# A two-layer hybrid attention and long-convolution step on one core: transposes, chunk order and handovers rearranged, two modulation chunks formed on another engine

## The reference

```
mod = silu(cond) @ w_ada + b_ada; sh1, sc1, g1, sh2, sc2, g2 = split(mod, 6)
h = x * (1 + sc1) + sh1
q, k, v, z, gate_a, gate_b = split(h @ w_in)
attn = softmax with a sink over |i-j| <= 128 (latent queries also read all context keys), rotary on q, k
x0, x1, u = split(depthwise_conv3(z)); g = the implicit filter of the layer, from a small sine MLP
hy = x0 * (irfft(rfft(x1 * u) * rfft(g)) + bias * (x1 * u))
merged = sigmoid(gate_a) * (attn @ w_pa) + sigmoid(gate_b) * (hy @ w_pb)
x = layer_norm(alpha * x + g1 * (merged @ w_out))
gate, val = split((x * (1 + sc2) + sh2) @ w_up)
x = layer_norm(alpha * x + g2 * ((gelu(depthwise_conv3(gate)) * val) @ w_down))
```

## Time and profile before

| quantity | value |
|---|---|
| median of 3 runs | 2078.3 us (2069.81 to 2085.46) |
| the profiled execution | 2079.39 us |
| its span | 2077.6 us |
| mean granted TensorE clock | 0.990 |

### The profile page before, as it was taken

How to read it: one execution, slowest core, us unless ns; L and a number is a source line. 1 busy time by engine, 2 the same in 40 slices (tenths; PEclk the granted TensorE clock), 3 DMA queues, 4 the chain that set the end, 5 groups by cost and what they waited for, 6 DMA issues and landing times.

```text
span 2077.6 us, 30343 instructions
## 1 busy us (share of the span) xinstructions
PE 2021.1 (97%) x13030; PEld 1920.9 (92%) x13030; DVE 1144.3 (55%) x1678; ACT 747.4 (36%) x1099; POOL 183.3 (9%) x202
## 2 busy tenths in 40 slices
PE   8999999999999999999999999999999999999997
PEld 3588998999989999999998999799998999999996
DVE  6416556867565777767544555763346533233435
ACT  3444344522255331233234444362226332133323
POOL 0120001200033000000022000120014000000011
PEclk9999989999999999999999999999999999999998
DMA  8331113245412435443322101222221221222121
GB/s 311 143 126 58 39 42 112 71 152 184 142 61 82 163 119 196 163 162 134 112 84 82 48 35 62 93 75 71 96 83 41 82 75 57 90 74 81 63 71 51
DMA packets 37726, 207.07 MB, mean 100 GB/s; under 512 B 4326, under 2 KB 7959, under 8 KB 18904
## 3 DMA queue, kind: packets, MB, share of 16 engines
q1 hardware_dynamic: 31192, 185.04, 24.8%
q0 software_dynamic: 3312, 13.35, 1.8%
q10 hardware_dynamic: 3088, 6.75, 0.9%
HBM read 196.98 MB, written 8.14 MB: 99 GB/s over the span
## 4 chain that ended last, share of the span: by engine, by line
PE 89%; DVE 4%; ACT 3%; issue 2%; DMA 1%; POOL 1%; SPq 0%; ACTq 0%; DVEq 0%; POOLq 0%
PE gemm_psum L608 50%; PE gemm_psum L638 15%; PE gemm_psum L661 4%; PE gemm_psum L681 3%; PE aux_psum L740 3%; PE gemm_psum L621 2%; PE aux_psum L793 2%; PE gemm_psum L550 2%; PE gemm_psum L779 2%; PE aux_psum L727 1%; PE gemm_psum L514 1%; PE aux_psum L763 1%; PE aux_psum L717 1%; DMA ada_early<-in_ada 1%; DVE scores L1626 1%
## 5 line engine op out<-in xcount | busy, mean ns | idle before, releaser
L608 PE MATMUL gemm_psum<-h_hi,w_hi 128*128 128x322 f32 x2176 | 504.6, 313 | 0.2 <-DVE gate_acc L1763 0.2
L608 PE MATMUL gemm_psum<-h_hi,w_lo 128*128 128x322 f32 x2176 | 500.8, 311 | 0.0
L608 PE MATMUL gemm_psum<-h_lo,w_hi 128*128 128x322 f32 x2176 | 498.9, 310 | 0.0
L1558 DVE TENSOR_TENSOR w_lo<-w_raw,w_hi 128x2048 fp32r<-128x2048 f32 (+4 forms) x134 | 260.4, 1943 | 218.2 <-ACT w_hi L1087 217.2
L608 PEld LDWEIGHTS gemm_psum<-h_hi,w_hi 128*128 128x128 f32 x2176 | 368.0, 189 | 4.7 <-issue 3.8
L608 PEld LDWEIGHTS gemm_psum<-h_lo,w_hi 128*128 128x128 f32 x2176 | 367.7, 189 | 0.0
L608 PEld LDWEIGHTS gemm_psum<-h_hi,w_lo 128*128 128x128 f32 x2176 | 367.4, 189 | 0.0
L1087 ACT ACTIVATE w_hi<-w_raw 128x2048 fp32r<-128x2048 f32 (+4 forms) x134 | 217.2, 1621 | 170.4 <-PE gemm_psum L638 65.6
L1546 DVE CUSTOM_DVE_ANT_0 aux_psum<-w_raw,cond_by_row 128x1024 f32<-128x1024 f32 x160 | 190.9, 1255 | 4.5 <-DMA w_raw<-in_ada_t 4.3
L1692 DVE SCALAR_TENSOR_TENSOR x<-gemm_psum,mod,x 128x128 f32<-128x128 f32 (+2 forms) x144 | 55.4, 434 | 160.6 <-PE gemm_psum L638 130.9
L638 PE MATMUL gemm_psum<-act_hi,w_lo 128*128 128x322 f32 x616 | 141.9, 311 | 0.0
(11 more groups left out here) (323 smaller groups left out, 3253.5 us busy)
## 6 DMA issues: line engine op xcount, KB each, us to landing
w_raw<-in_w_up SPq DMA_DIRECT2D x44, 1024.0 KB, 4.8
w_raw<-in_ada_t SPq DMA_DIRECT2D x40, 1024.0 KB, 4.7
w_raw<-in_w_down SPq DMA_DIRECT2D x32, 704.0 KB, 4.1
w_raw<-in_w_gate SPq DMA_DIRECT2D x16, 1024.0 KB, 4.7
w_raw<-in_w_z SPq DMA_DIRECT2D x12, 1024.0 KB, 4.7
w_raw<-in_w_out SPq DMA_DIRECT2D x8, 1024.0 KB, 4.7
g_kept<-g_rows_out POOLq DMA_DIRECT2D x10, 512.0 KB, 2.9
ada_early<-in_ada SPq DMA_DIRECT2D x4, 1024.0 KB, 20.6
```

What stands on the lines that cost most here:

```text
L608: last = mm(gp[:, 2 * (t % 2) + hf, 0:HALF], w[:, off + P * kk:off + P * (kk + 1)], moving(kk, lo)[:, hf * HALF:(hf + 1) * HALF], start=kk ...
L1558: TT(wlo[s][:, 0:n], raw[STEP[(lane.layer, "g", g)] % 2][:, 0:n], f32(whi[s][:, 0:n]), ALU.subtract).then_inc(sem["w_split"], raised("w_sp ...
```

## The change

1. Chunks 6 and 7 of layer 0's first modulation are no longer matmuls on PE but eight products on DVE, between filter products. The stream order becomes 6, 4, 7, 5. Twelve transposes stay, and the last four columns of the second vector come from the products. The products go to a new SBUF tile, one behind the other.
2. The load of `cond_rows` moves from POOL's queue to ACT's, ahead of x's two, and its Silu from the attention part to between the filters.
3. Six rows of layer 1's filter spectra (from the fifth on) are emptied by DVE, not ACT, around the split of chunk 0, and several rows of ACT's copies are moved into the loop that makes h.
4. Chunks 1 and up1 are split in halves too.
5. Three heads of p are transposed ahead of z's second tile (two before); in the last block, which has one z tile, that tile is done in halves, with the transposes between. ACT copies p of heads 0 and 2 ahead of z's second tile. `attn_lo` of the block before comes after the score maxima, not among them.
6. Pair 0's spectrum goes to two banks of its own, `spectrum(2)` waits no more for `usp_out`, and `attn_projected(1)` does; `early_row(0)` and `(2)` move behind splits of y.
7. At LN1 the statistics of the second half come after six channel groups (four before), with splits, squares and sums in another order on ACT, DVE and POOL.

The core of the diff:

```diff
-    order = [(0, "pre", 0), (0, "pre", 1)] + [(0, "ada", s) for s in range(ADA_EARLY, ADA_FIRST)]
+    order = [(0, "pre", 0), (0, "pre", 1)] + [(0, "ada", s) for s in (6, 4, 7, 5)]
-HALVED = [0] + [at_g("gate", m) for m in range(1, EARLY + 1)] + [at_g("up", 0)]
+HALVED = [0, 1] + [at_g("gate", m) for m in range(1, EARLY + 1)] + [at_g("up", 0), at_g("up", 1)]
+    spec_bank = lambda r: ax[:, r, :] if r < 2 else gp[:, r % 4, :]
@@ PE, opening @@
-        filter_rows(1, 4, 6)
+        filter_rows(1, 4, 8)
         ada(4)
+        filter_rows(1, 8, 10)
         g_spectrum(0, 1)
-        filter_rows(1, 6, 8)
+        g_spectrum(0, 2)
         ada(5)
-        g_spectrum(0, 2)
-        filter_rows(1, 8, 10)
-        ada(6)
-        ada(7)
         g_spectrum(1, 0)
-        pe.wait_ge(sem["row_first"], 4)
+        pe.wait_ge(sem["row_first"], 3)
-        for t in range(2 * KD):
+        for t in range(2 * ADA_ROWS):
@@ PE, attention @@
-                tile(5 + b, 0, KD, 0, h_mov, "z_mm")
-                p_transposed(b, 0, 2)
                 if b + 1 < NB:
+                    tile(5 + b, 0, KD, 0, h_mov, "z_mm")
+                    for n in range(3):
+                        p_transposed(b, n)
                     if b:
                         pe.wait_ge(sem["at_lo"], due("at_lo", b))
                     tile(5 + b, 1, KD, KD * P, h_mov, "z_mm")
-                p_transposed(b, 2, NH)
-                pv(b, NH - 2)
-                pv(b, NH - 1)
+                else:
+                    z_half(5 + b, 0)
+                    for n in range(3):
+                        p_transposed(b, n)
+                    z_half(5 + b, 1).then_inc(sem["z_mm"], raised("z_mm"))
+                for n in range(3, NH):
+                    pv(b, n - 3)
+                    p_transposed(b, n)
+                for n in range(NH - 3, NH):
+                    pv(b, n)
@@ PE, spectral stage @@
-                if r >= 4:
+                if r >= 6:
                     pe.wait_ge(sem["usp_out"], due("usp_out", r - 3))
-            pe.wait_ge(sem["ut_out"], due("ut_out", 2))
+            pe.wait_ge(sem["ut_out"], due("ut_out", 5))
             spectrum(0, U_V[0])
-            pe.wait_ge(sem["ut_out"], due("ut_out", 5))
             attn_projected(0)
+            pe.wait_ge(sem["usp_out"], due("usp_out", 2))
             attn_projected(1)
@@ PE, LN1 @@
-                if kk == 3:
+                if kk == 5:
                     ln_stats(0, 1, due)
@@ ACT @@
+        act.dma_start(crow[:, :, :], A["cond_rows"]).then_inc(sem["cond_rows_in"], 16)
         act.dma_start(x[:, :, CTX], A["x_prompt"]).then_inc(sem["x_in"], 16)
         g_rows(0, 3, 4)
+        act.wait_ge(sem["cond_rows_in"], 16)
+        run(crow[:, :, :], crow[:, :, :], ACT.Silu).then_inc(sem["cond_rows"], 1)
         filter_hi(1, 0, 2)
-                act.wait_ge(sem["gs_ready"], 20)
+                act.wait_ge(sem["filt_out"], 20)
                     h_make(0, 0, d, SH1, SC1)
-                    g_rows(1, 2 + d, 3 + d)
-                    if d == 3:
+                    if d < 3:
+                        filter_hi(1, 7 + d, 8 + d)
+                    if d in (1, 2):
+                        g_rows(1, 1 + d, 2 + d)
+                    if d == 5:
                         split_halves(0)
-                split(1)
+                split_halves(1)
                     p_copy(i - 1, 0)
+                    p_copy(i - 1, 2)
+                if i == NB:
+                    z_rows(i, 0)
                 if p_ == 0:
-                    early_row(0)
                     act.wait_ge(sem["usp_mm"], due("usp_mm", 4))
 ...
                 if p_ == 0:
+                    early_row(0)
                     early_row(1)
                     split(gI)
+                if p_ == 1:
                     early_row(2)
+            split_halves(at_g("up", 0))
             for d in range(KD):
                 h_make(H_FFN, 0, d, SH2, SC2)
+                if d in (1, 2, 4, 5):
+                    square(0, (4, 5, 6, 7)[(1, 2, 4, 5).index(d)], 1)
-            split(at_g("up", 1))
+            split_halves(at_g("up", 1))
@@ DVE @@
+                if l and m == 1:
+                    dve.wait_ge(sem["cond_rows"], 1)
+                    ada_t(0, 6)
+                if l and n == 0:
+                    ada_t(0, 7)
+                if l and n == 1:
+                    first_modulation()
+        def g_rows_late(r0, r1):
+            for r in range(r0, r1):
+                dve.wait_ge(sem["gsp_mm"], 10 + r + 1)
+                V.tensor_copy(gst[:, GSP_PAIRS[r // 2], r % 2, :], gp[:, 2 + r % 2, :]).then_inc(sem["gsp_late"], 1)
@@ DVE, soft @@
-            if b:
-                dve.wait_ge(sem["at_lo"], now("at_lo"))
+            if b:
+                attn_lo(b - 1)
@@ DVE, layer 0 @@
+                g_rows_late(4, 8)
                 dve.wait_ge(sem["mask_done"], 1)
-                split_halves(0)
-                split(1)
+                split_halves(0, (0,))
+                g_rows_late(8, 9)
+                split_halves(0, (1,))
+                g_rows_late(9, 10)
+                split_halves(1)
@@ POOL @@
+                        if h == 0 and d == 3:
+                            pool.wait_ge(sem["gs_ready"], 20)
-                pool.dma_start(crow[:, :, :], A["cond_rows"]).then_inc(sem["cond_rows_in"], 16)
-                if d == 6:
+                if d == 4:
                     sum1(0, 6, 1)
```

More of the change, by code:

```diff
@@ L686, in both, with z_half @@
                             last.then_inc(sem[event], raised(event))
+        def z_half(g, hf):
+            t, s = TILES.index((g, 0)), slot_of(g)
+            if hf == 0:
+                ev, n = last_read[t - 2]
+                pe.wait_ge(sem[ev], due(ev, n))
+            for kk in range(KD):
+                for n, (w, src) in enumerate(((whi[s], hhi), (whi[s], hlo), (wlo[s], hhi))):
+                    last = mm(gp[:, 2 * (t % 2) + hf, 0:HALF], w[:, P * kk:P * (kk + 1)], src[:, kk, half(hf)],
+                              start=kk == 0 and n == 0, stop=kk == KD - 1 and n == 2)
+            return last
         h_mov = lambda kk, lo: (hlo if lo else hhi)[:, kk, :]
@@ L1220, in _ @@
                 run(two(dst), pair(t), ACT.Copy).then_inc(sem["qkv_out"], raised("qkv_out"))
-            if L == 0:
-                act.wait_ge(sem["cond_rows_in"], 16)
-                run(crow[:, :, :], crow[:, :, :], ACT.Silu).then_inc(sem["cond_rows"], 1)
             def z_rows(i, c):
@@ L1253, in _ @@
                 if i:
-                    for n in range(2, NH, 2):
+                    for n in range(4, NH, 2):
                         p_copy(i - 1, n)
@@ new lines, in first_modulation @@
+        def first_modulation():
+            dve.wait_ge(sem["params_in"], 16)
+            dve.wait_ge(sem["col_mm"], 2 * ADA_ROWS)
+            modulation(0, gp[:, 0, 0:2 * KD], b_ada(0))
+            split_at = 2 * ADA_ROWS - KD
+            pairs = lambda j0, j1: b_ada(1, j0, j1).unsqueeze(2).to_broadcast([P, j1 - j0, 2])
+            STT(mod[:, KD:KD + split_at, :], gp[:, 0, 2 * KD:4 * ADA_ROWS].rearrange("p (j g) -> p j g", g=2), 1.0,
+                pairs(0, split_at), ALU.add, ALU.add).then_inc(sem["mlp_order"], 1)
+            n_ord[0] += 1
+            dve.wait_ge(sem["ada_t"], 4 * (ADA_FIRST - ADA_ROWS))
+            late = mod[:, KD + split_at:2 * KD, :]
+            dve.wait_ge(sem["mlp_order"], n_ord[0])
+            STT(late, late, 1.0, pairs(split_at, KD), ALU.add, ALU.add).then_inc(sem["mod_done"], raised("mod_done"))
@@ L1667, in tpv @@
                 scores(b + 1, 0, 2)
-                attn_lo(b)
         def attn_lo(b):
@@ L2272, in _layouts @@
     first = w_ada[0, :, :2 * D_MODEL].reshape(2, 4, P, 4, 512)
-    out["ada"] = np.ascontiguousarray(first.transpose(3, 0, 2, 1, 4)).reshape(ADA_FIRST, P, CHUNK)
+    out["ada"] = np.ascontiguousarray(first.transpose(3, 0, 2, 1, 4)).reshape(ADA_FIRST, P, CHUNK)[:ADA_ROWS]
     w_t = w_ada.transpose(0, 2, 1).reshape(D, ADA_STEPS, 2, P, D_MODEL)
```

141 lines of the change are left out of this document (67 added, 74 removed).

## The result

| | before | after |
|---|---|---|
| median of 20 runs | 2083.7 us (2069.0 to 2085.5) | 2068.0 us (2060.9 to 2075.0) |
| ratio, 95% interval | | 0.9942 (0.9927 to 0.9956) |
| profiled execution | 2079.4 us | 2074.6 us |
| mean granted TensorE clock | 0.990 | 0.990 |

The account below looks back on a forecast made before the run. PE was taken as the bound, busy 2021.1 of 2077.6 us. Terms of 12.6 + 7.4 + 10.4 + 3.1 + 0.9 = 34.4 off 2079.4 gave 2045, with an 8-in-10 range of 2034 to 2057.

Parts of the forecast that it names:

- the sentence on the load of `cond_rows`: Kernel start: moving this load to ACT's queue costs 0, as the whole queue landed by 45.2 and Silu needs it before 51.4.
- Rival (e): Kernel start: `cond_rows` lands late, from 51.4 on PE stops one for one, and the kernel gets slower; chance 0.02.
- Rival (f): Whole kernel: PE's gaps all reappear elsewhere, only its removed 7.0 us and some clock are gained, about 2068; chance 0.07.
- Opening: Layer 0's start through `opening`: removed matmuls and closed gaps leave 11.0 us, half clock gone 1.6, together 12.6.
- rival (d): Kernel's opening: DVE bounds it, the products don't fit between the filter's, only 2 of 12.6 us stay, 2056; chance 0.07.
- Attention: Attention blocks: `attn_lo` moved 2.8 us, block 0's `pv` gap 0.8, last block's gap 0.1; 3.7 a layer, 7.4 in both.
- Rival (b): Last attention block: half clock in both layers, by the transposes, 6.6 us more, 2051.6; chance 0.09.
- rival (a): Layer 0's last attention block: half clock absent since the gap preceding it is removed, 6.6 us less, 2038.4; chance 0.20.
- Spectral stage: Spectral stage: `u_spec` wait 2.45 us, half clock 1.5, `w_lo` wait 1.27 gained; 5.2 a layer, 10.4 in both.
- rival (c): Spectral stage: PE waits at `inverse` instead of `spectrum`, 9 of the 10.4 us are lost, 2054; chance 0.13.
- LN1: First layer norm: 0.65 us a layer from shorter gaps and 1.8 of clock in layer 0, together 3.1.
- LN2: Second layer norm: splitting chunk 1 in halves overlaps ACT and DVE, 0.9 us gained.

Follow-up runs that it names:

- ones_moved_timed: The changed kernel with the load of `ones` on SP's queue, not ACT's: 2048.4 us, ratio 0.9849 (2050.6 in an earlier single execution).
- pool_load: The changed kernel with the load of `cond_rows` on POOL's queue behind par, not on ACT's: 2048.8 us, ratio 0.9858.
- spectral_undone: The changed kernel with the load of `ones` on SP's queue, and the spectral stage as in the kernel before: 2053.1 us, ratio 0.9881.
- ln1_undone: The changed kernel, `ones` loaded by SP, DVE's copy 1 ahead of chunk 10's split, with LN1 as in the kernel before: 2042.4 us, ratio 0.9818.

## Why the prediction was wrong, step by step

- **The step that failed** is the sentence on the load of `cond_rows`: its cost was taken as 0, since the queue was empty at 45.2 and the new load lies ahead of x. This counts only when a transfer lands. The issue is an instruction of ACT, and the tenth one stood for 21.4 us. The prediction gave the moved load no price as an instruction of ACT. Rival (e), the only one about this load, priced its landing (needed by 51.4; it landed at 8.44 + 25.9 = 34.3, as forecast) and named ACT idle at 51 as its sign; the idle stood at 10. The step's size is 19.4 us net, and with it 2045 becomes 2064; the median was 2068. The rest is the 3.4 us by which the other terms together were too large (last bullet). Rival (f) names 2068 itself, but as "all of PE's gaps reappear elsewhere"; they didn't (without the stall 31 of 34.4 us were there), so its number is a coincidence.
- **Opening.** Forecast 11.0 us up to `opening`; 12.0 without the stall (12.08 to 111.64 is 99.56, 11.94 to 99.48 in `ones_moved_timed` is 87.54). Where the 1.0 more comes from isn't resolved. PE's idle time before `opening` was 0.97, forecast 0.9. The half clock behind it gave 1.55, forecast 1.6. The products were covered (rival (d) fell).
- **Attention.** Forecast 3.7 us a layer. From the second group of `qk` to tile (9,1) at full clock, layer 1 took 131.89 us before (1157.57 to 1289.46) and 129.97 in `pool_load` (1136.90 to 1266.87): 1.9. `attn_lo` was mis-sized, 1.5 instead of 2.8, and block 0's gap fell from 1.06 to 0.53, 0.5 instead of 0.8. That the last block's gap only moves one head on was right, 1.22 against a forecast 1.4.
- **The clock of the last block.** Rival (b), half clock in both layers, is what the profiled execution of the kernel after shows (by luck of the execution: `pool_load` and `ones_moved` have it in layer 0 alone, `spectral_undone` in none), and its reason, the transposes, was wrong. The same three transposes ran at full clock in all eight last blocks of the changed order that had no wait of PE. So the rule of the Trainium skill ("TensorE: Matmul & The Clock Gate", Part 4: PE-mode transpose), that full clock doesn't engage on transposes, isn't what decided here. My argument against rival (a), that layer 1 of before had both the gap and full clock, showed only that the gap isn't sufficient; I read it as if the gap didn't matter, and so missed that moving one DVE copy was worth 8 us.
- **Spectral stage.** Forecast 5.2 us a layer; 5.5 and 5.4 in the two traces, 5.7 when undone. Right in size and in each of the three pieces; rival (c) fell.
- **LN1, LN2.** LN1: forecast 3.1, measured about 1. The 0.65 a layer for the gaps isn't there (0.1 in layer 1 of the two traces, −0.2 in layer 0 of `ln1_undone`). The 1.8 of clock is real where it occurs, but it occurred in three of ten, and the sum took it as certain. LN2: forecast 0.9, measured 0.8.
- **Sum.** Without the stall 31 us of the 34.4 are there (`ones_moved_timed`): attention gave 1.8 a layer less than its term and LN1 2 less, opening 1 more. The range's end of 2057 was too near: it left no room for a moved instruction with a price that no row of before could show.

## What to carry to other kernels

A load that is moved to a compute engine's queue costs that engine the time of its issue, and the issue can block: count the loads issued in a row there, and leave what stands behind them in the engine's order nothing urgent. When a kernel's executions spread over 15 us in steps, look for the stretch whose clock differs between two layers of one profile, and take away the wait ahead of it, even one of 1.2 us: here one copy of DVE in another place gave a steady 2040 instead of 2041 to 2056. And a wait that is removed is worth only what the next one in the same chain leaves; at LN1 3.7 us of it a layer gave about one in both layers together, and that one was clock.

## What the runs showed of the hardware

- The tenth load issued in a row from ACT (2 MB each time) stood 18 to 21 us on its issue, whether a load of 1 MB or one of 32 bytes had been put ahead of it, and 12 us when it came at 19.15: the stand ended at 31.0 to 31.2 in these three kernels with `cond_rows` on the queue, at 28.0 in the one with 32 bytes in its place. Nine issues took 0.4 to 0.8 us each.
- TensorE's clock was at half speed (1.2 GHz) for most of a stretch of 15 us behind a wait of 1.2 to 1.5 us amid short transposes and 64-column matmuls in 12 of 18 cases, and in none of ten with waits of at most 0.25 us. The block costs 6.5 us more then (15.2 us from `pv`(1) to the next tile, against 8.7 in layer 1 of `pool_load`).
